# The final norm of a two-block kernel: its first token half scaled inside the last feed-forward stage by ScalarE and GpSimd, roots by square root and reciprocal, smaller stores

## What is computed

```python
def rms_norm(x, gain=None):
    xf = x.astype(F32)
    y = xf * lax.rsqrt(jnp.mean(xf * xf, axis=-1, keepdims=True) + NORM_EPS)
    if gain is not None:
        y = y * gain.astype(F32)
    return y.astype(x.dtype)
```

## Time and profile before

| what | us |
|---|---|
| median of 3 runs | 3507.95 |
| lowest and highest | 3506.53, 3509.79 |
| profiled execution, its own time | 3508.18 |
| span of its instructions | 3506.1 |
| busy PE, DVE, ACT, POOL | 3262.6, 1879.7, 1203.9, 653.3 |

### The profile page before, as it was taken

One profiled execution on the slowest core, in us unless ns is written; L12 is line 12 of the kernel. 1 busy time (PEld: TensorE's weight loads), 2 busy tenths in 40 slices (PEclk: granted clock), 3 DMA queues, 4 the chain that ended last, 5 costly groups with the idle time before them and its releaser, 6 DMA issues. The chain is left out here.

```text
span 3506.1 us, 38398 instructions
## 1 busy us (share of the span) xinstructions
PE 3262.6 (93%) x15060; PEld 2438.4 (70%) x15060; DVE 1879.7 (54%) x2863; ACT 1203.9 (34%) x1878; POOL 653.3 (19%) x616
## 2 busy tenths in 40 slices
PE   7999999998999999999998988987888899999997
PEld 4476554545787878888886866664466678888785
DVE  6546645555233464444476544354765485565558
ACT  3325622223322343333234232542220253333444
POOL 2100000000100045453001010010000025454442
PEclk7999999996999999999999999998989899999998
DMA  5430000001333122224774132233324132232865
GB/s 224 181 132 13 10 25 25 25 1 55 138 97 144 69 85 81 85 87 154 265 297 150 44 100 64 82 116 124 103 72 156 48 114 97 100 113 95 273 228 171
DMA packets 124763, 389.24 MB, mean 111 GB/s; under 512 B 15751, under 2 KB 33159, under 8 KB 109352
## 3 DMA queue, kind: packets, MB, share of 16 engines
q1 hardware_dynamic: 86872, 267.32, 21.9%
q0 software_dynamic: 21056, 111.05, 8.5%
q10 hardware_dynamic: 16656, 8.42, 1.3%
HBM read 312.17 MB, written 74.58 MB: 110 GB/s over the span
## 5 line engine op out<-in xcount | busy, mean ns | idle before, releaser
L1620 PE MATMUL banks<-work,weight_ring 128*128 128x512 f32 (+1 forms) x640 | 265.0, 560 | 5.4 <-ACT x L1710 4.9
L2224 POOL TENSOR_TENSOR quad_raw<-quad_raw 128x512 f32<-128x512 f32 x160 | 233.6, 1461 | 125.1 <-DMA quad_raw<-in_w_gu 118.9
L2356 PE MATMUL banks<-block_t_high,quad_low 128*128 128x512 f32 x608 | 236.6, 389 | 0.0
L1620 PEld LDWEIGHTS banks<-work,weight_ring 128*128 128x128 f32 x640 | 115.9, 190 | 115.0 <-issue 104.5
L2509 ACT ACTIVATE quad_partial<-banks 128x512 f32<-128x512 f32 x160 | 95.6, 598 | 247.0 <-PE banks L2356 236.6
L1820 DVE SCALAR_TENSOR_TENSOR x<-x,work,banks 128x128 f32<-128x128 f32 x320 | 111.3, 348 | 128.3 <-PE banks L1656 119.8
L2354 PE MATMUL banks<-block_t_high,quad_high_b 128*128 128x512 f32 x456 | 177.5, 389 | 0.1
L2355 PE MATMUL banks<-block_t_low,quad_high_b 128*128 128x512 f32 x456 | 177.4, 389 | 0.0
L2356 PE MATMUL banks<-block_b_high,quad_low 128*128 128x512 f32 x456 | 177.4, 389 | 0.0
L3370 PE MATMUL banks<-mix_high,ring_parts 128*128 128x512 f32 x320 | 135.7, 424 | 13.3 <-ACT work L3429 4.4
L2595 DVE TENSOR_TENSOR quad_gated<-banks,quad_partial 128x512 f32<-128x512 f32 x40 | 27.7, 691 | 217.8 <-PE banks L2356 211.2
(11 more groups left out here) (650 smaller groups left out, 8068.1 us busy)
## 6 DMA issues: line engine op xcount, KB each, us to landing
quad_raw<-in_w_gu SPq DMA_DIRECT2D x40, 768.0 KB, 4.2
condition_space<-in_mod_w POOLq DMA_DIRECT2D x24, 1024.0 KB, 7.0
pair_raw<-in_w_down SPq DMA_DIRECT2D x22, 1024.0 KB, 5.1
down_raw<-in_w_down SPq DMA_DIRECT2D x33, 512.0 KB, 4.5
columns_raw<-ffn_blocks SPq DMA_DIRECT2D x33, 512.0 KB, 5.7
weight_ring<-in_w_merge SPq DMA_DIRECT2D x24, 512.0 KB, 3.6
quad_raw<-in_w_gu SPq DMA_DIRECT2D x48, 256.0 KB, 3.0
weight_ring<-in_dft SPq DMA_DIRECT2D x12, 1024.0 KB, 5.1
```

Source lines behind the costliest of these rows:

```text
L1620: mm = e.matmul(pg.ps[:, bank_of(h, n), 0:b - a], slot[:, (2 * k + t) * P:(2 * k + t + 1) * P], h1[:, k, a:b], start=(k == 0), stop=(k == ...
L2224: e.tensor_tensor(self.weight(n, out), self.weight(n, a), self.weight(n, b), op).then_inc(self.sums.sem, 1)
L2356: mm = e.matmul(bank, w_lo[:, k], hi[:, k], start=False, stop=(k == 3), skip_group_check=again)
```

## The change

The function `norm_last` goes, and a class `LastNorm` takes its place, with parts that are called from the last feed-forward stage and parts in the norm's stage.

- Roots: ACT does one Sqrt from the bank (`sqrt`), and DVE one `reciprocal` on 128x512 (`reciprocal`), in place of Ln and Exp. A one-element Sqrt is put behind step 36 of ACT's list (`table`).
- First half, all inside the feed-forward stage: DVE does the reciprocal ahead of the adds of squares of step 38, and scales tile 0 behind them. For tiles 1 to 7 ACT multiplies x by the gain (`take_gain`, Identity with a scale), in between the squares of places 10 to 12, and POOL multiplies the result by the root factor in place (`first_on_pool`).
- Second half, in the norm's stage: DVE does the reciprocal and scales tiles 0 to 5; tiles 6 and 7 are multiplied by the gain on ACT at the end of the feed-forward stage and by the root factor on POOL.
- Stores: ten instead of four, of one or two tiles (256 or 512 KB), each behind the tiles that it needs. SP takes them in the order first half, then second half.

```diff
+class LastNorm:
+    ON_VECTOR, SECOND_ON_POOL = 1, 2
+    def __init__(self, pg, gain):
...
+        self.first = Mem(pg.big, M_H + 2 * T, M_END)(KT, HALF)
+        self.second = Mem(pg.big, M_H + 6 * T, M_END)(KT, HALF)
...
+    def table(self, e):
+        e.activation(self.pg.silu_c[:, 0, 0:1], self.pg.eps, ACT.Sqrt)
+    def sqrt(self, e, s, bank):
+        self.of_half.ms.wait(e, s + 1)
+        e.activation(self.of_half.rs[:, s, :], bank, ACT.Sqrt, bias=self.pg.eps[:, 0:1], scale=1.0 / D).then_inc(self.logs.sem, 1)
+    def reciprocal(self, e, s):
+        self.logs.wait(e, s + 1)
+        rs = self.of_half.rs[:, s, :]
+        e.reciprocal(rs, rs).then_inc(self.of_half.rt.sem, 1)
+    def scale(self, e, s, tiles, sem):
+        self.of_half.rt.wait(e, s + 1)
+        for k in tiles:
+            e.scalar_tensor_tensor(out=(self.first, self.second)[s][:, k, :], in0=self.pg.x[:, k, s * HALF:(s + 1) * HALF], scalar=self.gain(k),
+                                   in1=self.of_half.rs[:, s, :], op0=ALU.mult, op1=ALU.mult).then_inc(sem.sem, 1)
+    def take_gain(self, e, s, tiles):
+        for k in tiles:
+            e.activation((self.first, self.second)[s][:, k, :], self.pg.x[:, k, s * HALF:(s + 1) * HALF], ACT.Identity,
+                         bias=self.pg.zero_col[:, 0:1], scale=self.gain(k)).then_inc(self.gained.sem, 1)
+    def on_pool(self, e, s, tiles):
+        self.of_half.rt.wait(e, s + 1)
+        for k in tiles:
+            v = (self.first, self.second)[s][:, k, :]
+            self.gained.wait(e, k - self.ON_VECTOR + 1 if s == 0 else KT - self.ON_VECTOR + k - tiles[0] + 1)
+            e.tensor_tensor(v, v, self.of_half.rs[:, s, :], ALU.mult).then_inc(self.by_pool.sem, 1)
...
+        def sync(e):
+            self.scaled.wait(e, 1)
+            store(e, 0, 0, 1)
+            for k, n in ((1, 1), (2, 2), (4, 2), (6, 2)):
+                self.by_pool.wait(e, k + n - 1)
+                store(e, 0, k, n)
+            for k in (0, 2, 4):
+                self.scaled.wait(e, 1 + k + 2)
+                store(e, 1, k, 2)
+            for k in (6, 7):
+                self.by_pool.wait(e, KT - 1 + k - 5)
+                store(e, 1, k, 1)
...
     (ffn_blocks, pool: behind the last step)
+        pg.last_norm.first_on_pool(e)
     (ffn_blocks, scalar)
+            if n == 36:
+                pg.last_norm.table(e)
             if n == 38:
-                take_squares(e, 8, 12)
-        squares.roots.root(e, 0, pg.ps[:, 7, :])
+                take_squares(e, 8, 10)
+        pg.last_norm.sqrt(e, 0, pg.ps[:, 7, :])
+        pg.last_norm.take_gain(e, 0, (1, 2))
+        take_squares(e, 10, 11)
+        pg.last_norm.take_gain(e, 0, (3, 4, 5))
+        take_squares(e, 11, 12)
+        pg.last_norm.take_gain(e, 0, (6, 7))
         take_squares(e, 12, 16)
+        pg.last_norm.take_gain(e, 1, (6, 7))
     (ffn_blocks, vector)
             if n == 38:
+                pg.last_norm.reciprocal(e, 0)
                 for i in range(8, 12):
                     squares.add(e, i)
+        pg.last_norm.scale(e, 0, range(pg.last_norm.ON_VECTOR), pg.last_norm.scaled)
         added.wait(e, 2)
```

More of the change, by code:

```diff
@@ L1051, in modulation_first, with first_on_pool, stage, pool @@
              vector=in_turn(lb_terms, weave(filt["vector"], vector), lb_bounds, filt["stored"]))
[L1054 to L1069, removed]
+class LastNorm:
+    ON_VECTOR, SECOND_ON_POOL = 1, 2
+    def __init__(self, pg, gain):
+        self.pg, self.gain = pg, gain
+        self.of_half = Roots(pg, pg.squares, pg.scratch(2, HALF))
+        self.first = Mem(pg.big, M_H + 2 * T, M_END)(KT, HALF)
+        self.second = Mem(pg.big, M_H + 6 * T, M_END)(KT, HALF)
+        self.logs = pg.shared_sem("norm_logs", 2)
+        self.gained = pg.shared_sem("norm_high", KT - self.ON_VECTOR + self.SECOND_ON_POOL)
+        self.scaled, self.by_pool = pg.shared_sem("norm_scaled", self.ON_VECTOR + KT - self.SECOND_ON_POOL), pg.shared_sem("norm_split", KT - self.ON_VECTOR + self.SECOND_ON_POOL)
+    def table(self, e):
[22 more added lines that the diff above has]
+            e.tensor_tensor(v, v, self.of_half.rs[:, s, :], ALU.mult).then_inc(self.by_pool.sem, 1)
+    def first_on_pool(self, e):
+        self.on_pool(e, 0, range(self.ON_VECTOR, KT))
+    def stage(self, name, stored):
+        pg, bank = self.pg, self.pg.ps[:, 1, :]
+        last = KT - self.SECOND_ON_POOL
+        def pool(e):
+            self.on_pool(e, 1, range(last, KT))
+        def vector(e):
+            self.reciprocal(e, 1)
+            self.scale(e, 1, range(last), self.scaled)
+        def store(e, s, k, n):
+            src = (self.first, self.second)[s][:, k:k + n, :]
+            e.dma_start(pg.out[:, k:k + n, s * HALF:(s + 1) * HALF], src).then_inc(stored, 16)
+        def sync(e):
[10 more added lines that the diff above has]
+                store(e, 1, k, 1)
+        pg.stage(name=name, sync=sync, gpsimd=pool, tensor=lambda e: self.of_half.sum(e, 1, bank),
+                 scalar=lambda e: self.sqrt(e, 1, bank), vector=vector)
+        return 10 * 16
@@ L4527, in block_2 @@
 def block_2(pg):
-    x, h = pg.x, pg.h2
-    half = lambda v: (lambda s: v[:, :, s * HALF:(s + 1) * HALF])
+    x = pg.x
     m = SsdMemory(pg)
@@ L4635, in block_2 @@
         lambda k: pg.sc2b[:, k:k + 1], lambda k: pg.mod2[:, 24 + k:25 + k])
+    pg.last_norm = LastNorm(pg, lambda k: pg.col("final_g", k))
     pg.stored = pg.sem("output_stored")
[L4638 to L4644, removed]
+    pg.stored_all = pg.last_norm.stage("norm_final", pg.stored)
 def block_2_layout(l0, o, gu):
@@ L4732, in _ @@
             e.wait_ge(pg.stage_done, 3 * stages[-1]["until"])
-            e.wait_ge(pg.stored, 64)
+            e.wait_ge(pg.stored, pg.stored_all)
         @block.gpsimd
```

## The result

| | before | changed |
|---|---|---|
| median of 13 runs each, taken in turns, us | 3504.03 | 3514.35 |
| ratio, with its 95% interval | | 1.0028 (1.0019 to 1.0037) |
| span of the profiled execution, us | 3506.1 | 3512.7 |

The kernel became slower by 0.28%, 9.8 us at 3504, with 6.6 to 13.0 inside the interval. The forecast was 3516.0 with 3511.5 to 3519.0, that is 8.0 more than the median of before that was known then (3507.95 of 3 runs).

What follows compares the result with a forecast made beforehand. DVE's chain to the last squares, then sum, roots, scales and 5.0 us of stores bound the end: last add 3496.6, sum 3498.8, roots 3503.0, scales 3509.15, span 3514.1, 8.0 added to median 3507.95: 3516.0, range 3511.5 to 3519.0.

Steps and rivals of the forecast that it cites:

- Reciprocals: DVE, one per half, 3.35 us each; second half's roots 4.2 us against 4.01 before, so nothing won.
- POOL beside DVE: Adds of squares beside POOL's seven products: each turn costs DVE 1.04 us, last add 4.1 us later, at 3496.6.
- (b): Rival at POOL's products beside DVE: POOL costs DVE nothing, time 3509.9; chance 0.09.
- (c): Rival at evictions from PSUM: they yield to POOL too, seven turns of 1.04 us, time 3519.2; chance 0.11.
- (a): Rival at adds 10 to 14: semaphore-dependent adds pay only half a turn each, time 3513.0; chance 0.18.
- (e): Rival beside POOL: DVE kept out for the whole 1.29 us, six turns, time 3517.5; chance 0.05.
- 2.35 us of the first reciprocal: DVE, ahead of step 38's adds: without POOL's effect, last add at 3492.5 instead of 3490.16, all on the path.
- ACT and its table: ACT: one Sqrt table load of 1.28 us hidden behind step 36; gains about 0.63 to 0.8 us each, ready before needed.
- The sum on PE: PE, behind the last add: 2.04 us at half clock instead of 1.32, after 10 us idle, ending 3498.8.
- Scales: DVE, second half: six scales of 0.663 us plus 0.08, with two turns of POOL between, ending 3509.15.
- 5.0 us behind the last scale: Kernel's end: last stores of 1 MB, issued from 3509.2 with the queue empty of the first half, span end 3514.1.
- two turns of 1.04: DVE's second-half scales: POOL's two products there each hold DVE up 1.04 us, 2 x 1.04 within the scales.

Runs made afterwards that it cites:

- roots alone: Kernel before with Sqrt on ACT and reciprocal on DVE instead of Ln and Exp, both halves, nothing else; ratio to before 1.0023.
- small stores: Kernel before with eight stores of two tiles instead of four of four; span ends 24.1 us behind DVE's last split, 25.3 before.
- the start moved: Changed kernel, POOL's second-half products wait for tiles 0 and 1, tiles 6 and 7 stored second; span ends 28.9 us behind PE's end, 28.1 in changed.

## Why the prediction was right, and where not

The split of step 38 ended 1.74 us earlier in the changed kernel's trace than in before's, so I put 1.74 us onto its times to compare them with the forecast's.

- **Reciprocals.** Forecast 3.35 us from 3480.7; measured 3.34 from 3480.71. Right, and that the second takes the place of Exp and the loads and wins nothing too: from the sum's start to the first scale 6.33 us now, 2.04 + 4.2 forecast.
- **POOL beside DVE.** Forecast 3496.6 for the last add; measured 3496.69. The pattern came turn by turn: first add free, then POOL in between, evictions untouched, 0.3 us of wait at the twelfth square, 1.29 us over the last three. Leaving POOL's products out brought 4.4 us back (4.1 in the sum), moving an operand to PSUM 4.0. So the rivals of no cost (b), of evictions that yield (c) and of half turns (a) are out, and the whole 1.29 us for each turn (e) too: an add beside POOL took 0.9 us more and the scale of tile 0 1.0 us more.
- **The two costs aren't independent.** The 2.35 us of the first reciprocal were worked out without POOL: with POOL's products left out it cost 2.0 (5.9 against 3.9), with them 3.1 (10.3 against 7.2). The sum of both was right, 6.5 forecast and 6.5 measured.
- **ACT and its table.** One load, behind step 36 as forecast, none later; Square, Identity and Sqrt ran on it. The gains took 0.80 us each (0.63 to 0.8 forecast) and stay hidden. That they stand ahead of the barrier was not seen; it costs 0.5 us as soon as DVE is quicker.
- **The sum on PE.** 2.04 forecast, 2.05 measured; with PE kept busy 1.28.
- **Scales.** 6.15 us forecast, 6.17 measured.
- **The step that was wrong.** "5.0 us behind the last scale", taken for 1 MB behind it with the queue empty. The number was 5.1, but by chance. The queue wasn't empty: at the last scale the stream of the second half had been running for some 1.7 us, and 1.5 of the 2.1 MB were still to come. What decides is the start of that stream, whether it is fed (7.7 us from its first issue to the end of the span in three runs without a gap), and, when POOL works late, the drain of POOL's queue, 7.0 us behind its last product, a term that the sum didn't have. In the changed kernel it had 1 us to spare. By the run without it POOL's help in the second half costs 2.2 us, and not 0.8 as by the sum (two turns of 1.04 against two scales of 0.663), and the order of the last stores is worth nothing.
- **The total.** Tail +8.0 forecast, +8.4 measured; 3516.0 forecast, 3514.35 measured. That the absolute time is this close is in part luck: the median of before came out at 3504.03 in the 13 runs, 3.9 us under the 3507.95 that I started from, and the difference came out at 9.8 (ratio) where I had added 8.0. One part I had priced at nothing: smaller stores let the stream begin two scales earlier, a gain of 1.2 us when done alone; what they bring inside the changed kernel no run shows.

## What to carry to other kernels

Work that is moved from a full engine to an idle one is no gain while the two share something: here seven products on POOL slowed DVE at the very place that set the end, and one operand in PSUM spared 3.6 of the 8.4 us. Before moving work, ask what stands between the last input and the last output: a slower instruction on the bounding engine (reciprocal for Exp) costs its whole length, while the same time on a free engine was covered. Where a long stream of stores ends a kernel, its first store and its gaps count, not its last. And look at when each queue ends, not only the one that stores: here POOL's queue needed 7.0 us behind its last product, so products given to it near the end can become the end.

## What the runs showed of the hardware

- PE's clock after the last matmul: the granted clock fell from 2.4 to 1.2 GHz 3.8 us behind PE's end in one run and 4.6 us behind it in before. The sum started after 3.92 us of idle time in before and took 1.32 us; after 3.80 us in the run with roots alone and took 2.05, after 3.94 us with small stores and took 1.69, the clock falling within it. So idle time alone doesn't tell which side an instruction falls on; in before the fall came 0.7 us after the sum had begun. The fall in the run with roots alone (columns as above, the clock is the third from the right):

```profile
3490.00:3491.00 1.00, 0.00 (x0) 0.00 (x0) 0.90 (x2) 0.37 (x1) 0.00 (x0) 1.00 0.00 0
3491.00:3492.00 1.00, 0.62 (x1) 0.50 (x2) 0.79 (x2) 0.00 (x0) 0.00 (x0) 0.69 0.00 0
```

- Between the last data of the stream of stores and the end of the span lie 0.9 to 1.4 us in twelve traces, and 2.4 and 2.9 us in the two in which POOL waited for DVE in the last stage and its drain came last.
- The drain that closes POOL's queue ends 7.0 to 7.1 us behind POOL's last product in all 14 traces, whether that product came 4 us (the start moved) or 33 us (before) ahead of the last data of the stores.
- A reciprocal of 128x512 f32 on DVE takes 3.35 us, five times an add; POOL was idle beside each one seen.
